# One level of Strassen's scheme for the feed-forward's lower product, summed in PSUM

## The reference

```python
h = h + rmsnorm(y, g_post_mix[l])
m = rmsnorm(h, g_pre_ffn[l])                                    # (1024, 1024) for the tokens kept
m = jnp.square(jax.nn.relu(m @ w_ffn_up[l])) @ w_ffn_down[l]    # 1024 -> 4096 -> 1024
h = h + rmsnorm(m, g_post_ffn[l])
```

## Time and profile before

| | |
|---|---|
| median of 3 runs (all) | 1603.17 us (1597.62, 1603.17, 1606.47) |
| span of the profiled execution | 1596.8 us |
| PE busy | 1510.9 us (95%) |
| DVE busy | 1037.1 us (65%) |
| ACT busy | 749.8 us (47%) |
| POOL busy | 181.1 us (11%), none of it in the last stage |
| DMA | 186.24 MB, mean 117 GB/s |
| granted clock | mean 0.981 of full |

### The profile page before, as it was taken

How to read it: one execution, slowest core, us unless ns; L and a number is a source line. 1 busy time by engine, 2 the same in 40 slices (tenths; PEclk the granted TensorE clock), 3 DMA queues, 4 the chain that set the end, 5 groups by cost and what they waited for, 6 DMA issues and landing times. The chain is left out here.

```text
span 1596.8 us, 37107 instructions
## 1 busy us (share of the span) xinstructions
PE 1510.9 (95%) x15576; PEld 1280.7 (80%) x15576; DVE 1037.1 (65%) x1598; ACT 749.8 (47%) x1317; POOL 181.1 (11%) x235
## 2 busy tenths in 40 slices
PE   6999999978999999999699989999999999999997
PEld 6999999977677777777478868888888888888886
DVE  6243545436888788798766685555555766667766
ACT  6254535426777787787645453333334111111132
POOL 6232344331011010110000000000000000000000
PEclk9999999997999999999899999999999999999999
DMA  4434462564523232220434454233332323223335
GB/s 178 147 125 146 156 230 97 208 179 155 112 50 81 61 87 55 50 50 13 132 81 132 163 173 158 106 113 113 117 120 103 116 92 93 92 93 106 93 105 185
DMA packets 89181, 186.24 MB, mean 117 GB/s; under 512 B 7856, under 2 KB 47920, under 8 KB 88768
## 3 DMA queue, kind: packets, MB, share of 16 engines
q1 hardware_dynamic: 84496, 167.50, 33.5%
q10 hardware_dynamic: 3744, 13.85, 2.2%
q0 software_dynamic: 784, 2.65, 0.7%
HBM read 125.20 MB, written 57.49 MB: 114 GB/s over the span
## 5 line engine op out<-in xcount | busy, mean ns | idle before, releaser
L689 PE MATMUL inproj_acc<-xn_xl,inproj_wh 128*128 128x348 f32 (+1 forms) x384 | 123.5, 322 | 0.0
L689 PE MATMUL inproj_acc<-xn_xh,inproj_wl 128*128 128x348 f32 (+1 forms) x384 | 123.3, 321 | 0.0
L689 PE MATMUL inproj_acc<-xn_xh,inproj_wh 128*128 128x348 f32 (+1 forms) x384 | 123.3, 321 | 0.0
L2352 DVE TENSOR_TENSOR all_mh_f<-all_mh_f,tail_bank 128x512 f32<-128x512 f32 x112 | 76.8, 686 | 52.3 <-PE tail_bank L2506 50.4
L2352 DVE TENSOR_TENSOR all_ml_f<-all_ml_f,tail_bank 128x512 f32<-128x512 f32 x112 | 76.8, 686 | 51.9 <-PE tail_bank L2506 51.9
L2506 PE MATMUL tail_bank<-all_mh,tail_tl 128*128 128x512 f32 x256 | 100.9, 394 | 0.0
L2506 PE MATMUL tail_bank<-all_mh,tail_th 128*128 128x512 f32 x256 | 100.9, 394 | 0.0
L2506 PE MATMUL tail_bank<-all_ml,tail_th 128*128 128x512 f32 x256 | 100.9, 394 | 0.0
L2506 PE MATMUL tail_bank<-tail_th 128*128 128x512 f32 x256 | 99.8, 390 | 0.3 <-DVE tail_tl L2253 0.3
L2506 PE MATMUL tail_bank<-tail_tl,tail_th 128*128 128x512 f32 x256 | 99.9, 390 | 0.0
L2506 PE MATMUL tail_bank<-tail_th,tail_tl 128*128 128x512 f32 x256 | 99.7, 389 | 0.0
(11 more groups left out here) (353 smaller groups left out, 4423.8 us busy)
## 6 DMA issues: line engine op xcount, KB each, us to landing
tail_raw<-in_w_up SPq DMA_DIRECT2D x32, 512.0 KB, 4.5
u_scratch<-tail_c SPq DMA_DIRECT2D x64, 256.0 KB, 2.1
tail_raw_d<-in_w_down SPq DMA_DIRECT2D x32, 512.0 KB, 3.7
tail_raw_u<-u_scratch SPq DMA_DIRECT2D x32, 512.0 KB, 3.3
xn_raw<-in_w_in SPq DMA_DIRECT2D x27, 512.0 KB, 4.8
p_scratch<-inproj_out ACTq DMA_DIRECT2D x26, 520.0 KB, 2.7
chunk_scratch<-inproj_fields SPq DMA_DIRECT2D x4, 2720.0 KB, 12.2
mix_swp<-chunk_scratch SPq DMA_DIRECT2D x32, 256.0 KB, 5.1
```

Of the source, the lines that this page charges most:

```text
L689: last = pe.matmul(acc[g][:, 0:size], w[s][:, kt, :], xx[:, kt, col:col + size], start=(kt == 0 and j == 0), stop=(kt == KD - 1 and j == 2))
L2352: dve.tensor_tensor(acc(t, g), acc(t, g), downs[o % 4][:, :], ALU.add).then_inc(added, 1)
```

## The change

The lower product C = U W (1024 tokens x 4096 hidden x 1024) is cut in two along every dimension, the hidden one alternately by tile (f = 0, 1 of each chunk), and computed with seven products instead of eight (Winograd's form, four sums on each side). Each of the seven is a pass of 8 chunks, summed over the chunks in four PSUM banks; the passes alternate between two sets of four banks. DVE adds each pass's four tiles into the output quadrants that it belongs to (`evict`). The sums of hidden tiles are made by DVE (`hidden_sums`) during the upper product and stored with three of the four tiles; the sums of `w_down` are made by GpSimd (`quad_sums`): SP loads four blocks (1 MiB), GpSimd overwrites them with four sums, SP stores them to a new DRAM tensor `d_dram`, 16 times, two in each of the first four turns (and before them), then one a turn. The operands of a chunk (512 KB of U, 512 KB of W) are loaded to three raw buffers and split into four pairs of operand buffers, the first in `mh`/`ml`, three in `th`/`tl`. The end is done by half rows, with the first-finished half squared earlier.

```diff
+DOWN_CHUNKS = FF_TILES // FC // 2
+DOWN_PASSES = [(U_A11, False, B_11), (U_A12, False, B_21), (U_S2, True, D_2), (U_S3, True, D_3), (U_S1, True, D_1),
+               (U_S4, False, B_22), (U_A22, True, D_4)]
+W_BEFORE = [[0, 1], [2, 3], [4, 5], [6, 7], [8, 9]] + [[i] for i in range(10, 2 * DOWN_CHUNKS)]
+W_DURING = [[0, 1], [2, 3], [4, 5], [6, 7]] + [[i] for i in range(8, 2 * DOWN_CHUNKS)]
...
-        downs = [bank[6], bank[7], bank[1], bank[4]]
+        downs = [[bank[6], bank[7], bank[1], bank[4]], [bank[0], bank[3], bank[2], bank[5]]]
+        op_high = [tiles(b) for b in (x_block(mh, 0, 1), th[:, T2], th[:, T3], th[:, T1])]
+        OUTS = TOK_TILES // 2
+        SPLIT = CHUNKS_ALL - len(op_high)
+        evict_at = {DOWN_CHUNKS * (i + 1) + 2: i for i in range(PASSES - 1)}
...
             turn(*of(TOK_TILES - 1))
             load_x(T4, 1, 0, slice(0, HALF))
-            for f in range(FC):
-                for k in range(2):
-                    store(0, f, k)
+            product.wait(sp, "plain", PLAIN_ORDER[-1])
+            for i in W_BEFORE[0]:
+                load_quad(i)
+            for f, k in ((0, 0), (1, 0), (1, 1)):
+                store(0, f, k)
             for q in range(1, LASTP + 1):
+                low.wait(sp, A22, q - 1)
                 if q < LASTP:
-                    low.wait(sp, A22, q - 1)
                     load_w(q + 1)
...
+                if q == LASTP - 1:
+                    sp.wait_ge(c_stored[0, 0], 16 * q)
+                    load_down(0)
+                if q == LASTP:
+                    load_down(1)
+                for i in W_DURING[q - 1] if q <= len(W_DURING) else []:
+                    store_quad(i)
                 store(q, 0, 0)
                 if q > 1:
                     store(q - 1, 1, 0)
+                store_sums(q - 1)
+                for i in W_BEFORE[q] if q < len(W_BEFORE) else []:
+                    load_quad(i)
                 store(q, 1, 1)
...
+            def load_down(c):
+                left, made, right = DOWN_PASSES[pass_of(c)]
+                n, b = c % DOWN_CHUNKS, c % len(down_raw)
+                if c >= len(down_raw):
+                    sp.wait_ge(down_low, 2 * (c - len(down_raw) + 1))
+                sp.dma_start(down_raw[b][:, 0, :], u_dram[left, n]).then_inc(down_loaded[b], 16)
+                sp.dma_start(down_raw[b][:, 1, :], (d_dram if made else w_down)[right, n]).then_inc(down_loaded[b], 16)
...
+            def quad_sums(i):                                    # GpSimd
+                b = lambda k: w_quads[i % 2][:, k, :]
+                done = lambda ins, k: pool_sums.done(ins, "D", k, i)
+                pool.wait_ge(quad_loaded[i % 2], 16 * (i // 2 + 1))
+                done(pool.tensor_tensor(b(D_1), b(B_12), b(B_11), ALU.subtract), D_1)
+                pool_sums.wait(pool, "D", D_1, i)
+                done(pool.tensor_tensor(b(D_3), b(B_22), b(B_12), ALU.subtract), D_3)
...
+            def hidden_sums(q):                                  # DVE, after c21(q) in turn q+1
...
+                done(dve.tensor_tensor(u(0), c_of(0, 1, q), c_of(1, 1, q), ALU.add), 0)
+                done(dve.tensor_tensor(u(2), c_of(0, 0, q), c_of(0, 1, q), ALU.subtract), 2)
+                hid_sums.wait(dve, "S", 0, q)
+                done(dve.tensor_tensor(u(1), u(0), c_of(0, 0, q), ALU.subtract), 1)
+                hid_sums.wait(dve, "S", 1, q)
+                done(dve.tensor_tensor(u(3), c_of(1, 0, q), u(1), ALU.subtract), 3)
...
+            def of_chunk(c):                                     # ACT; from c = 4 on it waits for PE's chunk c-4
...
+                for j in range(2):
+                    act.activation(op_high[b][:, j, :], down_raw[c % len(down_raw)][:, j, :], ACT.Copy).then_inc(down_high, 1)
...
+            for c in range(3, CHUNKS_ALL):                       # DVE
+                low_of_chunk(c)
+                if c in evict_at:
+                    for o in range(OUTS):
+                        evict(evict_at[c], o)
+                if SPLIT - 1 <= c < SPLIT + 3:
+                    finish(c - SPLIT + 1)
             for o in range(OUTS):
+                evict(PASSES - 1, o)
+                finish(OUTS + o)
...
+            def down(c, o, signal=True):                         # PE
...
                 for f in range(FC):
+                    own_tile = slice(f * HALF + o * P, f * HALF + (o + 1) * P)
                     for j, (u, w) in enumerate(((uh, dh), (uh, dl), (ul, dh))):
+                        last = pe.matmul(downs[pass_of(c) % 2][o][:, :], u[:, own_tile], w[:, f * HALF:(f + 1) * HALF],
+                                         start=(n == 0 and f == 0 and j == 0), stop=(n == DOWN_CHUNKS - 1 and f == FC - 1 and j == 2))
...
             for o in range(OUTS):
+                for c in range(SPLIT, CHUNKS_ALL):
+                    chunk_ready(c)
+                    down(c, o, c == CHUNKS_ALL - 1)
```

More of the change, by code:

```diff
@@ L1969, in first @@
                 relu_squared(plain[j][:, :], f, k, 0)
-            def down_high(n):
-                if n == 0:
-                    product.wait(act, "plain", 3)
-                elif n == 1:
-                    product.wait(act, 7, LASTP)
-                else:
-                    act.wait_ge(down_done, (n - 1) * OUTS)
-                for f in range(FC):
-                    act.wait_ge(d_loaded[f], 16 * (n + 1))
-                    act.activation(dh[n % 2][:, f, :], raw_d[f][:, :], ACT.Copy).then_inc(d_high, 1)
@@ new lines, in square_early @@
+            def square_early(t):
+                act.wait_ge(evicted, (OUTS if t < OUTS else 4 * OUTS) + t % OUTS + 1)
+                if t:
+                    act.wait_ge(early_done, 2 * t)
+                else:
+                    product.wait(act, 4, LASTP)
+                act.activation(square[:, :], early(t), ACT.Square, accum_out=ss_early[:, t:t + 1]).then_inc(early_done, 1)
+                act.wait_ge(early_done, 2 * t + 1)
+                act.activation(eps_early[:, t:t + 1], ss_early[:, t:t + 1], ACT.Identity, scale=1.0 / D, bias=eps).then_inc(early_done, 1)
@@ new lines, in root_late @@
+            def root_late(t):
+                act.wait_ge(evicted, (5 if t < OUTS else 6) * OUTS + t % OUTS + 1)
+                act.wait_ge(early_done, 2 * TOK_TILES)
+                if t:
+                    act.wait_ge(late_done, 3 * t)
+                act.activation(square[:, :], late(t), ACT.Square, accum_out=ss_late[:, t:t + 1]).then_inc(late_done, 1)
+                act.wait_ge(late_done, 3 * t + 1)
+                act.activation(out_rs[:, t:t + 1], ss_late[:, t:t + 1], ACT.Ln, scale=1.0 / D,
+                               bias=eps_early[:, t:t + 1]).then_inc(late_done, 1)
+                act.wait_ge(late_done, 3 * t + 2)
+                act.activation(out_rs[:, t:t + 1], out_rs[:, t:t + 1], ACT.Exp, scale=-0.5).then_inc(late_done, 1)
@@ L2325, in _ @@
                 c11(q)
+                if q == 1:
+                    hidden_sums(0)
                 if q < LASTP:
@@ L2330, in _ @@
                     c21(q - 1)
+                    hidden_sums(q - 1)
                     of_raw(A22, q, 1, 1, -1.0)
                 if q == LASTP - 1:
-                    for f in range(FC):
-                        down_low(0, f)
+                    low_of_chunk(0)
                 if q < LASTP:
@@ L2337, in _ @@
                 else:
-                    for f in range(FC):
-                        hidden_low(0, f)
+                    low_of_chunk(1)
                 c22(q)
@@ L2371, in _ @@
-            for f in range(FC):
-                down_low(LAST, f)
-            for f in range(FC):
-                hidden_low(LAST, f)
-            dve.wait_ge(gain_loaded, 16)
+                half = lambda g: slice(g * HALF, (g + 1) * HALF)
+                g_early = t // 4
+                g_late = 1 - g_early
+                scratch = gained_late[t % 2][:, :]
+                dve.wait_ge(evicted, (5 if t < OUTS else 6) * OUTS + t % OUTS + 1)
+                dve.wait_ge(gain_loaded, 16)
@@ L2376, in _ @@
+            low_of_chunk(2)
+            c21(LASTP)
+            hidden_sums(LASTP)
+            for c in range(3, CHUNKS_ALL):
+                low_of_chunk(c)
[4 more added lines that the diff above has]
+                    finish(c - SPLIT + 1)
             for o in range(OUTS):
-                add(LAST - 1, o)
-                if o % 2 == 1 and o > 1:
-                    finish(o // 2 - 1)
```

339 lines of the change are left out of this document (194 added, 145 removed).

## The result

| | before | after |
|---|---|---|
| median of 4 runs each | 1601.07 us | 1583.46 us (1580.66 to 1584.78) |
| ratio after to before | | 0.9897 (95%: 0.9877 to 0.9918) |
| span of the profiled execution | 1596.8 us | 1581.9 us (its own time 1583.7) |
| PE busy | 1510.9 us | 1477.3 us |
| DMA volume | 186.24 MB | 257.53 MB |

The change makes the kernel 17.6 us (1.1%) faster. Forecast were 36 us. The sign is right, and more than half of the gain is missing. The time lies in the wide range (1551 to 1590), but outside 1556 to 1582, the part of it that the prediction gave to its own mechanism.

What follows compares the result with a forecast made beforehand. The prediction took the lower product to be bound by its number of matmuls, with PE busy throughout the upper too. -46.3 + 0.5 - 2 + 6 + 4 + 2 = -36 us (rounded) gave 1567 us, range 1556 to 1582 (wide 1551 to 1590).

Steps and rivals of the forecast that it cites:

- Added in the upper product: Upper product: late weight loads and DVE meeting GpSimd add +6, +4 and +2 us.
- The next three double turns: Upper product, turns after the first: at 350 GB/s weights land 5 to 7 us late, +1.3 each, +4 us together.
- Turn 1, "+6" for the weights behind two groups: Upper product, turn 1: two groups (2 MiB) queue before a weight load that has no room, +6 us.
- DVE and GpSimd, "+2": Upper product: DVE operations meeting GpSimd pay about 1.0 us each, mostly hidden; +2 us in four double turns, bounds 0 and +42.
- Matmuls removed: Lower product: 1344 matmuls instead of 1536, -46.3 us, all on the path.
- The lower product is fed: Lower product: loads at 191 GB/s keep PE supplied; 0.5 us for the last four chunks, bounds 0 and 3.
- rival 4: Lower product starves if a load takes 14 us: +34, about 1600 us; chance 0.05.
- The end: Behind the last matmul: half rows instead of whole rows, -2 us, bounds 0 and -3.
- DMA rate: Upper product: 350 GB/s taken; single turns (258 GB/s) fit easily, double turns (367 GB/s) just don't.
- rival 2: Upper product: DMA becomes the bound, at 230 GB/s +65, 1620 us; chance 0.07.
- Rival 3: Upper product: GpSimd's lock holds DVE in every turn, +42, about 1597 us; chance 0.10.
- Rival 1: Upper product takes all added work for nothing, +0 to 2, 1555 us; chance 0.21.

Runs made afterwards that it cites:

- e4: Changed kernel with SP asking for upper weights ahead of the next groups, but still behind the store that waits for GpSimd; 1585.62 us.
- e12: e4 with the stores of the groups' sums moved behind the weights' load too, so SP never waits for GpSimd before it; 1566.09 us.
- e7: Changed kernel with its SP order, but one group a turn and only 12 of 16 made, plain w_down read for the rest; 1556.30 us.
- e8: Kernel before the change, with 4 to 18 extra copies ahead of u2 in six turns; PE idle 0.58 to 9.39 us lengthened turns by 0.82 to 12.09 us.
- e1: Changed kernel without groups: none loaded, summed or stored, plain w_down read instead of sums; 1548.49 us.
- e2: Changed kernel with all group transfers kept, but each GpSimd sum on one column instead of 512; 1558.00 us.
- e3: Changed kernel with all GpSimd sums made, but only the first two groups loaded and none stored; 1556.19 us.
- e11: e5 with the first two groups loaded ahead of turn 1, as early as in the changed kernel, upper weights before them; 1559.55 us.
- e5: Changed kernel, weights first, three group buffers, start in turn 1, two groups at most every second turn, later stores, A22's low part before hidden_sums; 1548.60 us.
- e10: e5 with two groups in each of turns 1 to 5 in a row; 1558.30 us.
- e6: Changed kernel with GpSimd issuing the loads and stores of its groups in its own queue, SP none; 1592.26 us.

## Why the prediction was wrong, step by step

**The step that failed is "Added in the upper product":** +12 forecast, +35.4 measured. It has three terms and one that it lacks. The measured 35.4 are +8.9 in "first", +23.5 in turns 2 to 5, and +3.1 in turns 6, 8 and 9 (one group each), which the forecast put at nothing; the turns before took 0.1 over theirs.

1. *The next three double turns, "+4".* Measured +23.5 over 19.30 in turns 2 to 5 (3.4, 8.2, 7.1, 4.8; some 2 us of turn 2 are the clock behind the stall before it). The prediction followed the volume through the queue, at 350 GB/s, and priced the queue right (7.1 us measured in turn 3, 5 to 7 forecast). It did not follow SP's own program, in which the weights' load stands behind the store of the last groups, and that behind GpSimd. Shown by e4 and e12: with the load ahead of the groups but behind that wait nothing is gained; with the wait moved behind the load as well, the length falls by 19.6 us against e4 and by 15.9 against the changed kernel. The wait moved by itself was not run. e7 shows the same from the other side: with one group a turn the round trip fits the turn.
2. *Not in the sum: the clock.* Stalls were priced at their idle time. e8 shows that four of six bring 1.9 to 2.7 us on top, and the profile after has 11.1 us of it (12.4 with what a stall costs beyond its idle time anyway), spread over the terms above and below. The Trainium skill ("TensorE: Matmul & The Clock Gate", "What's actually happening") says that the low clock is the default state and that only activity releases it; the trace agrees (0.50 behind a pause of 5.62 us), and the rule should have stood in the forecast beside every stall that it counted.
3. *Turn 1, "+6" for the weights behind two groups.* Measured +8.9, not far in size, but by luck: the reason is another. Counted from the first matmul, ACT casts those weights only 1.8 us later than before (955.51 - 915.38 against 952.32 - 913.99). e1 has 1.6 of the 8.9 without any group; e2 (transfers alone) has 2.6 more than e1, e3 (sums alone) 7.3; e11 (weights ahead) has 7.8 more than e5. It is GpSimd beside DVE: in turn 1 DVE also makes low parts of x sums over 2048 columns, which I did not look for, and which take 3.36 us instead of 2.29 here:

```profile
945.10 2.29 DVE L2350 TENSOR_TENSOR tail_tl<-tail_tl_f,tail_th 128x2048 fp32r<-128x2048 f32 x1
947.31 1.78 DVE L2302 TENSOR_TENSOR tail_al_f<-tail_raw,tail_al_f 128x512 f32<-128x512 f32 x1
949.13 3.33 DVE L2284 TENSOR_TENSOR tail_al<-tail_al_f,tail_ah 128x512 fp32r<-128x512 f32 x2
952.38 3.36 DVE L2350 TENSOR_TENSOR tail_tl<-tail_tl_f,tail_th 128x2048 fp32r<-128x2048 f32 x1
955.66 1.75 DVE L2284 TENSOR_TENSOR tail_al<-tail_al_f,tail_ah 128x512 fp32r<-128x512 f32 x1
...
966.52 1.28 DVE L2280 TENSOR_TENSOR tail_al<-tail_raw,tail_ah 128x512 fp32r<-128x512 f32 x2
```

   DVE works without a gap from the first of these rows to the last, which is what PE stands for before product 1 of turn 2. The four `hidden_sums` (0.68 us each) lie in that chain too, just ahead of the last row. The prediction had looked for their room in the later turns only; e1, which has them, shows no such stall.

4. *DVE and GpSimd, "+2".* Price as forecast: DVE's 0.69 us becomes 1.75, +1.06 each (forecast +1.0), and GpSimd's operation, alone and beside DVE, takes

```profile
984.70 1.30 POOL L1963 TENSOR_TENSOR tail_w_quad<-tail_w_quad 128x512 f32<-128x512 f32 x1
986.07 1.60 POOL L1965 TENSOR_TENSOR tail_w_quad<-tail_w_quad 128x512 f32<-128x512 f32 x1
```

The trace agrees with the exclusive lock of the Trainium skill ("SBUF — State Buffer", "SBUF: two separate sides") as the prediction weighed it. What was wrong is how often it bites. In turn 1 it was not looked for and costs 7.3 us (e3 over e1). In the double turns the place was right, DVE's nine operations from product 5 to product 6, but the size was not: where the weights are in time, PE does wait at their end, 6.0 us in three times in e12 and 8.0 in four in e10, which with the clock makes 8.3 and 10.9 us of length for "+2". In the changed kernel this lies hidden behind the weights: there PE never waits before product 6 of a double turn.

**What was right.** *Matmuls removed:* -46.3 + 0.5 forecast, -48.5 measured, with no idle time and the clock at 1.00. The 2 us more are the distance of the matmuls from `mh` (see the last section). *The lower product is fed:* DMA at 215 GB/s (191 forecast), u loads land in 3.7 us; rival 4 is out. *The end:* 9.7 us from the end of the last matmul to the span's end before, 6.6 after: -3.1 for -2. *DMA rate:* the stretch behind the stall above moves 322 GB/s, e5 moves more in the same time with 2.8 us of loss over e1, and three of the six turns with one group are at 19.30; rival 2 is out. By the 358 GB/s of the Trainium skill ("DMA: Bandwidth & Descriptors", "Specifications") the double turns would have been 0.5 us longer each; no run here shows that limit apart from the waits for DVE. *Rival 3*, the lock in every turn, is out by e3, where three turns with two groups and five with one are at 19.30; where the sums do meet DVE's chain, as in e10, up to 5.1 us of its 7.8 are paid. *Rival 1*, "all for nothing", was wrong for this kernel, but 1555 us is within 7 us of what e1 and e5 show to be possible.

Sum: -48.5 - 3.1 + 35.4 + 1.4 (the stage starts at 915.4 instead of 914.0) = -14.8, and the spans differ by 14.9. The medians differ by 17.6, within the runs' spread.

**Open:** why the idle time of 2.47 us in e8 cost only 0.27 beyond itself when 1.84 cost 1.86; why e6 keeps the weights late; how much of the 8.3 us in e12's turns 4 to 6 is DVE beside GpSimd and how much the store that DVE waits for in one of them; which of e5's parts that were not taken back matter.

## What to carry to other kernels

When a side job is threaded into a tuned loop, follow the issuing engine's program, not only its queue's bytes: every load that the critical chain needs must stand ahead of the side job's transfers and ahead of its waits, and the first move showed nothing here without the second. Price each stall of the matmul engine at its idle time and some 2 us of lower clock on top. Start and spread the side job where the other engines' chains have room (here one turn later, and at most every second turn with two groups), even if these engines end up busier.

## What the runs showed of the hardware, unexpected

- Behind pauses of 1.84, 3.73, 5.62 and 9.39 us PE ran 8 to 13 of the matmuls right behind at half clock, 0.427 us apart instead of 0.227, at a granted clock of 0.58, 0.60, 0.50 and 0.50 (the twelve behind the pause); behind 2.47 us it stayed at 1.00, and that pause and one of 0.58 us cost 0.27 and 0.24 beyond themselves.
- The distance of 0.233 us is no property of `mh` as a buffer. With both operands in `mh`/`ml`, 12 lower matmuls take 2.73 us, and 12 of the upper product, with `mh` and `tail_ah`, 2.80 right behind them:

```profile
1264.04 0.39 PE L2652 MATMUL tail_bank<-all_mh 128*128 128x512 f32 x1
...
1266.77 0.40 PE L2582 MATMUL tail_bank<-all_mh,tail_ah 128*128 128x512 f32 x1
...
1269.57 0.39 PE L2652 MATMUL tail_bank<-all_mh 128*128 128x512 f32 x1
```

- DVE at 268 of 292 us (92%) beside GpSimd at 102 costs PE next to nothing (2.8 us of length over e1) when the sums are spread as in e5; the same sums two groups a turn cost 8.4 us more (e10).
